# Order of the stick-breaking heads and the square root in a two-layer hybrid block: values placed behind the next block's first scores

## The chip, the cores and the metric

One Trainium2 chip, one core. The metric is the device time of one execution, in microseconds (us); lower is better. The engines are PE (TensorE; its weight loads are PEld), DVE (VectorE), ACT (ScalarE), POOL (GpSimd) and SP (SyncE, which here only issues transfers).

## The reference, cut to what matters

A two-layer model on 528 tokens (16 of them "meta" tokens) of width 1024. Layer 0 mixes with a state-space group and retention, layer 1 with stick-breaking attention and a gated linear recurrence; a convolutional feed-forward part follows each. The change is in the mixer of layer 1:

```python
def stick_breaking_attention(q, k, v):            # 16 heads of 64
    ...
        z = jnp.einsum('bqhd,bkhd->bhqk', q, k) * scale
        strict = jnp.arange(s1)[None, :] < jnp.arange(s0, s1)[:, None]
        log_1m = jnp.where(strict, jax.nn.log_sigmoid(-z), 0.0)
        after = lax.cumsum(log_1m, axis=3, reverse=True) - log_1m
        w = jnp.where(strict, jnp.exp(jax.nn.log_sigmoid(z) + after), 0.0)
        outs.append(jnp.einsum('bhqk,bkhd->bqhd', w, v))

def rg_lru(x, w_a, b_a, w_x, b_x, lam):           # 8 blocks of 128 channels
    r = sigmoid(x @ w_a + b_a); i = sigmoid(x @ w_x + b_x)
    log_a = -LRU_C * r * softplus(-lam)
    a = exp(log_a)
    b = jnp.sqrt(jnp.maximum(-jnp.expm1(2.0 * log_a), 0.0)) * (i * x)
    # h_t = a_t * h_(t-1) + b_t over the tokens

u = h @ w_in;  q, k, v, gate, xr = split_cols(u, ...)
y = concat([attention, rg_lru(conv(xr)) * gelu(gate)]) @ w_out
```

## The kernel before

Activations are kept transposed, channels on partitions and the 528 tokens along the free dimension. Every dense product is done in three passes, high part times high part, high times low and low times high. A **unit** is one 128-column block of a weight: SP brings it to `raw`, ACT writes its rounded part to `whi` (L661), DVE the rest to `wlo` (L1059), and PE multiplies it in `gemm` (L359) in eight **portions** of six matmuls (the index k). There are two buffers of each of these, so the ACT copy for unit u waits (in `split_hi`) until PE has finished unit u-2, and signals it only with the last matmul of that unit.

Layer 1's mixer runs in eight **blocks** n = 0 to 7. A block has two attention heads (e = 0, 1) and one 128-channel block of the recurrence. While PE multiplies the five units of the next block's projection (the five tiles q, k, v, gate, xr), the function `l1_small(i, b, unit, k)` puts the small products of this block behind given portions; (3, 1) means behind portion 1 of unit 3. PE executes all this in one fixed order. Before the change it is:

- (0, 2): `suffix(n-1, 1)`, the triangular sums of the second head of the block before (L549 to L561). They need the high and low parts that ACT and DVE make one after the other (`soft` on both engines).
- (0, 5): `values(n-1)`: the weights of both heads times the values (L571 for the 16 meta tokens, L576 for the rest), into bank 3 and a corner of bank 1 of the shared PSUM tile `small` (`sp_`).
- (0, 7): `gates(n)` (L586, L588), the two gate products of the recurrence.
- (1, 3): `v_out(n)` (L595, L597), transposing the values; then `scores(n, 0)` (L403, and the mask products of L537), the scores of the first head, into banks 0 to 2.
- (3, 1): `suffix(n, 0)`. (3, 4): `scores(n, 1)`.

ACT's order in a block, written out in `l1_block`: weight copy 1 (`split(1)`), `weigh(n-1, 1)` (L948, the exponential of the second head before), `l1_heads_out(n-1)` (L980, L981, results of `values` to `yT`), `lru_root(n-1)` (a table load and a square root at L995, and `load_exp` at L942, another table load with a one-column exponential), `l1_gates(n)` (L956 to L964), weight copy 2, `l1_v(n)` (L969, transposed values to `sv_tok`), then `soft(n, 0)`. In `soft` the absolute value and the exponential of the scores come first (L920 to L925), then what is called `between` (for the first head `l1_v_last` at L973 and weight copy 3, for the second weight copy 5), then a table load and the logarithms (L927, L929), then the high parts (L934 to L938). `load_exp`, `weigh(n, 0)`, weight copy 4, `soft(n, 1)` and `load_exp` end the block.

DVE's order: tile 4, the four-tap convolution for the recurrence (`lru_in`, L1096 and L1098), the low part of weight 1, `lru_out(n-1)` (L1577 to L1579, needs the square root), `gelu_in` (L1556 to L1558), the low part of weight 2, tile 0, weight 3, tile 1, `soft(n, 0)` (L1502 to L1529), `lru_var` (L1563 to L1567), and so on. `l1_gates(n)` waits for `lru_out(n-1)`, because they share buffers, and `v_out(n)` waits for the first part of `l1_gates(n)`.

In block 7 (`early=True`) the units beside it are those of the output projection; their right-hand side is made by `y_part` (ACT L835, DVE L1381) in the buffers `hn_hi` and `hn_lo`, with `weigh(6, 1)` inside it, and PE waits for it portion by portion. `suffix(7, 1)` and `values(7)` stand in the sixth unit of that projection.

Of the kernel before, what the change touches and what calls it, by code (L numbers as in the profile page):

```python
# [21 lines left out]
P = 128  # L22
# [14 lines left out]
NT = 5  # L37
# [10 lines left out]


V_LAST = ((1, 416), (2, 432))  # L50

# [68 lines left out]
def build(nc, x_h, vec_h, cst_h, dec_h, w_dt, w_ssd, w_ret, w_out0, w_fi0, w_fo0, w_l1, w_out1, w_fi1, w_fo1,  # L122
# [4 lines left out]
    with ctx:  # L127
# [3 lines left out]
        def sem(name):  # L131
            return ctx.enter_context(nc.semaphore(name))
# [24 lines left out]
        with scope() as mix:  # L157
# [38 lines left out]
            with scope() as s3:  # L196
                qs = [sb(f"qs{s}", [P, T], f32, s3) for s in range(2)]
                ks = [sb(f"ks{s}", [P, T], f32, s3) for s in range(2)]
                vs, gt, xc, tr = vr[:, 0, :], vr[:, 1, :], gr[:, 0, :], gr[:, 1, :]
                ubx = ub[:, 0, :]  # L200
                gw = [sb(f"gw{s}", [P, 2 * P], f32, s3) for s in range(2)]
                sv_tok = sb("sv_tok", [P, NT, P], f32, s3)
                lbuf = sb("lbuf", [P, CAUSAL], f32, s3)
                spb = sb("spb", [P, CAUSAL], f32, s3)
                sp_hi = sb("sp_hi", [P, CAUSAL], f32r, s3)
                sp_lo = sb("sp_lo", [P, CAUSAL], f32r, s3)
                later = sb("later", [P, LATER], f32, s3)


                spare = slice(KD * P, KH * P)  # L210
                later_hi = (whi[0][:, spare], sb("later_hi", [P, 416], f32r, s3)[:], whi[1][:, spare])
                later_lo = (wlo[0][:, spare], sb("later_lo", [P, 416], f32r, s3)[:], wlo[1][:, spare])
                wts = [sb(f"wts{s}", [P, CAUSAL], f32, s3) for s in range(2)]
                lt, lb = (sb(n, [P, T], f32, s3) for n in ("lt", "lb"))
                ge, ti, la = ub[:, 1, 3:3 + T], sq[:, 0, :], sq[:, 1, :]
                hb = sb("hb", [P, 2, 8], f32, s3)
                nsp = sb("nsp", [P, 8], f32, s3)
                nspt = sb("nspt", [P, 8], f32, s3)
# [20 lines left out]
        def pcol(name, c=0, n=1, rows=P):  # L239
# [36 lines left out]
            sem(n) for n in ("xc_done", "gates_done", "tri_done", "la_done", "lb_done", "root1_done"))  # L276
        z_done, l_done, spf_done, suf_done, w_done, pv_done = (
            sem(n) for n in ("z_done", "l_done", "spf_done", "suf_done", "w_done", "pv_done"))
        tvs_done, svtok_done, ysb_done, gu_done, gth_done, ylru_done = (
            sem(n) for n in ("tvs_done", "svtok_done", "ysb_done", "gu_done", "gth_done", "ylru_done"))  # L280
        sum_done, sphi_done, later_done, lathi_done, latlo_done = (
            sem(n) for n in ("sum_done", "sphi_done", "later_done", "lathi_done", "latlo_done"))
        prep_done, spl_done, spl_ln = sem("prep_done"), sem("spl_done"), sem("spl_ln")
# [63 lines left out]
        def _(pe):  # L347
# [181 lines left out]
            project(W_FO0, T_FO0, hid_hi, hid_lo, KH, (hlo_done, 0))  # L529


            def scores(n, b, e):

                rows = slice(HEAD * e, HEAD * (e + 1))
                causal([ks[b][rows, :]], [qs[b][rows, :]], None, once=True)
                for j, _, _, bk, c0, _ in (PIECES[0], *PIECES[2:]):
                    ins = pe.matmul(sp_[0:SZ[j], bk, c0:c0 + SZ[j]], ident_b[0:SZ[j], 0:SZ[j]],  # L537
                                    never[0:SZ[j], 0:SZ[j]], start=False, stop=True, skip_group_check=True)
                ins.then_inc(z_done, 1)
# [22 lines left out]
                                    stop=True, skip_group_check=True)  # L562
                ins.then_inc(suf_done, 1)

            def values(n):


                pe.wait_ge(w_done, 2 * n + 2)
                for e in range(2):
                    c = slice(HEAD * e, HEAD * (e + 1))  # L570
                    pe.matmul(sp_[c, 1, 32:32 + N_META], sv_tok[:, 0, c], wts[e][:, 0:N_META], start=True, stop=True)  # L571
                for j in range(NT):
                    q0 = max(N_META, P * j)
                    for e in range(2):
                        c = slice(HEAD * e, HEAD * (e + 1))
                        ins = pe.matmul(sp_[c, 3, q0 - N_META:512], sv_tok[0:SZ[j], j, c],  # L576
                                        wts[e][0:SZ[j], OFF[j] + q0 - P * j:OFF[j] + WJ[j]], start=j == 0,
                                        stop=j == NT - 1, skip_group_check=True)
                ins.then_inc(pv_done, 1)

            def gates(n, b, half_n):
                wait_count(pe, ysb_done, n)
                pe.wait_ge(xc_done, n + 1)
                pe.wait_ge(gw_in[b], 16 * (half_n + 1))
                for gate, (b0, b1, c1) in enumerate(((0, 1, 0), (2, 1, 16))):
                    pe.matmul(sp_[:, b0, 0:512], gw[b][:, gate * P:(gate + 1) * P], xc[:, 0:512],  # L586
                              start=True, stop=True)
                    ins = pe.matmul(sp_[:, b1, c1:c1 + 16], gw[b][:, gate * P:(gate + 1) * P], xc[:, 512:T],  # L588
                                    start=True, stop=True)
                ins.then_inc(gates_done, 1)  # L590

            def v_out(n):

                for i in range(4):
                    pe.transpose(sp_[:, 3, P * i:P * (i + 1)], vs[:, P * i:P * (i + 1)], ident)  # L595
                for e, (bk, c0) in enumerate(V_LAST):
                    ins = pe.matmul(sp_[0:SZ[4], bk, c0:c0 + HEAD], vs[:, 512:T], ident[:, HEAD * e:HEAD * (e + 1)],  # L597
                                    start=True, stop=True)
                ins.then_inc(tvs_done, 1)

            def l1_small(i, b, unit, k):

                n = 2 * i + b
                before = not (isinstance(n, int) and n == 0)
                if (unit, k) == (0, 2) and before:
                    suffix(n - 1, 1)
                if (unit, k) == (0, 5) and before:
                    values(n - 1)
                if (unit, k) == (0, 7):
                    gates(n, b, i)  # L610
                if (unit, k) == (1, 3):
                    pe.wait_ge(tri_done, n + 1)
                    v_out(n)
                    scores(n, b, 0)
                if (unit, k) == (3, 1):
                    suffix(n, 0)
                if (unit, k) == (3, 4):
                    pe.wait_ge(w_done, 2 * n + 1)
                    scores(n, b, 1)

# [19 lines left out]
            for c in range(5, 8):  # L640
                def after(k):
                    if c == 5 and k == 2:
                        suffix(7, 1)
                    if c == 5 and k == 5:
                        values(7)
                hgemm(At(0, 0, W_OUT1 + c), At(0, 0, T_OUT1 + c), after=after)

            project(W_OUT1 + KD, T_OUT1 + KD, y_hi, y_lo, KD, (ylo_done, 3 * KD), per=1)
# [6 lines left out]
        def _(act):  # L655
# [257 lines left out]
            act.activation(nspt[:], nspt[:], ACT.Ln, bias=1.0).then_inc(spl_ln, 1)  # L913
            act.wait_ge(spl_done, 2)

            def soft(n, e, between):


                act.wait_ge(z_done, 2 * n + e + 1)
# [7 lines left out]
                act.activation(lbuf[0:SZ[4], FULL:CAUSAL], lbuf[0:SZ[4], FULL:CAUSAL], ACT.Ln, bias=1.0)  # L927
                for b, w, at in reversed(BANKS):
                    act.activation(lbuf[:, at:at + w], lbuf[:, at:at + w], ACT.Ln, bias=1.0).then_inc(l_done, 1)  # L929

                for k, (b, w, at) in enumerate(reversed(BANKS)):
                    act.wait_ge(sum_done, 3 * (2 * n + e) + k + 1)
# [30 lines left out]
                act.wait_ge(gu_done, n + 1)  # L963
                act.activation(ge, ge, ACT.Tanh, scale=GELU_C).then_inc(gth_done, 1)  # L964

            def l1_v(n):
                act.wait_ge(tvs_done, n + 1)
                wait_count(act, pv_done, n)
                act.activation(sv_tok[:, 0:4, :], sp_[:, 3, :].rearrange("p (i c) -> p i c", c=P), ACT.Copy)  # L969

            def l1_v_last(n):
                for e, (bk, c0) in enumerate(V_LAST):
                    ins = act.activation(sv_tok[0:SZ[4], 4, HEAD * e:HEAD * (e + 1)], sp_[0:SZ[4], bk, c0:c0 + HEAD],  # L973
                                         ACT.Copy)
                ins.then_inc(svtok_done, 1)

            def l1_heads_out(n):

                act.wait_ge(pv_done, n + 1)
                act.activation(yT[:, n, 0:N_META], sp_[:, 1, 32:32 + N_META], ACT.Copy)  # L980
                act.activation(yT[:, n, N_META:T], sp_[:, 3, :], ACT.Copy).then_inc(ysb_done, 1)  # L981

            def hb_col(gate, n):
# [14 lines left out]
            def l1_block(i, b, early=False):  # L998
# [7 lines left out]
                if early:  # L1006
                    act.wait_ge(unit_done, W_OUT1)
                    y_part(hn_hi, EARLY[1], W_OUT1, lambda: weigh(n - 1, 1))
                else:
                    split(1)  # L1010
                    if before:
                        weigh(n - 1, 1)
                if before:
                    l1_heads_out(n - 1)
                    lru_root(n - 1)
                l1_gates(n)
                split(2)
                l1_v(n)
                soft(n, 0, lambda: (l1_v_last(n), split(3)))
                load_exp()  # L1020
                weigh(n, 0)
                split(4)
                soft(n, 1, lambda: split(5))
                load_exp()

            for b in range(2):
                l1_block(0, b)
# [6 lines left out]
            l1_block(3, 1, early=True)  # L1034
            split_hi(At(0, 0, W_OUT1 + 6))
            weigh(7, 1)
            l1_heads_out(7)
            lru_root(7)
            split_hi(At(0, 0, W_OUT1 + 7))
            split_hi(At(0, 0, W_OUT1 + 8))  # L1040
            act.wait_ge(ysb_done, 8)
# [740 lines left out]
```

## Time and profile before

| | us |
|---|---|
| three runs, median (lowest, highest) | 1885.35 (1885.19, 1885.55) |
| the profiled execution | 1886.69 |
| its span | 1884.7 |
| PE busy | 1825.9 (97%) |
| DVE busy | 1221.8 (65%) |
| ACT busy | 755.5 (40%) |

The blocks of layer 1's mixer run from 1020 to 1430 us of the span. A timeline row gives the start, the time busy, the engine, the line, the operation with its output and inputs, the count of instructions merged in it, and in brackets how long the engine was idle before it and what it is taken to have waited for. A matmul's end is modelled and overlaps the next, so lengths on PE are best read from start to start.

### The profile page before, as it was taken

How to read it: one execution, taken by the hardware profiler on the slowest of the kernel's cores; microseconds unless marked ns; L12 is line 12 of the kernel's file. 1: busy time of each engine (PE TensorE's matmuls, PEld its weight loads, DVE VectorE, ACT ScalarE, POOL GpSimd, SP SyncE). 2: the span in 40 equal slices, each digit the busy share in tenths (PEclk: the TensorE clock that was granted, in tenths of full speed). 3: DMA queues.
4: the chain of work that ended last, by engine and by line, in shares of the span. 5: the costliest groups of instructions: out<-in, count | busy, mean ns of one | idle time of the engine just before them, and what ended most of it. 6: DMA issues, size and time to landing. Idle time of an engine off the chain costs nothing.

```text
span 1884.7 us, 36044 instructions
## 1 busy us (share of the span) xinstructions
PE 1825.9 (97%) x14286; PEld 1737.0 (92%) x14286; DVE 1221.8 (65%) x1740; ACT 755.5 (40%) x1135; POOL 68.5 (4%) x140
## 2 busy tenths in 40 slices
PE   7999999999999999999999999999899999999996
PEld 7999998999899999999998888888789999999996
DVE  7787756455456777774334777777775688878323
ACT  5444432121234222222224777777774422223221
POOL 0122220000000000000000000000000000000000
PEclk9999999999999999999999999999999999999998
DMA  4222213222222222232222111111112222223221
GB/s 150 91 80 79 90 49 111 68 68 67 68 71 86 89 89 89 89 97 95 90 78 72 58 59 49 59 58 59 57 45 79 89 89 89 89 89 102 93 92 60
DMA packets 39938, 149.92 MB, mean 80 GB/s; under 512 B 4384, under 2 KB 5408, under 8 KB 39216
## 3 DMA queue, kind: packets, MB, share of 16 engines
q1 hardware_dynamic: 38672, 142.16, 24.1%
q10 hardware_dynamic: 1184, 6.60, 1.0%
q8 instruction: 59, 0.97, 0.2%
q14 instruction: 23, 0.19, 0.0%
HBM read 146.62 MB, written 2.13 MB: 79 GB/s over the span
## 4 chain that ended last, share of the span: by engine, by line
PE 71%; issue 12%; DVE 9%; ACT 6%; POOL 2%; DMA 0%; DVEq 0%; ACTq 0%; POOLq 0%
PE gp L359 60%; PE small L403 3%; PE small L414 3%; DVE spb L1502 1%; DVE sp_lo L1524 1%; ACT lbuf L922 1%; DVE wlo L1059 1%; ACT lbuf L925 1%; PE small L576 1%; POOL dec L1664 1%; PE small L553 1%; ACT whi L661 1%; PE small L561 1%; ACT L927 1%; ACT L995 0%
## 5 line engine op out<-in xcount | busy, mean ns | idle before, releaser
L359 PE MATMUL gp<-hn_hi,whi 128*128 128x264 f32 x3216 | 664.6, 288 | 23.0 <-DVE wlo L1059 12.2
L359 PE MATMUL gp<-hn_hi,wlo 128*128 128x264 f32 x3216 | 657.4, 286 | 0.0
L359 PE MATMUL gp<-hn_lo,whi 128*128 128x264 f32 x3216 | 656.7, 286 | 0.0
L661 ACT ACTIVATE whi<-raw 128x1024 fp32r<-128x1024 f32 (+1 forms) x249 | 273.6, 1099 | 775.5 <-PE gp L359 774.5
L1059 DVE TENSOR_TENSOR wlo<-raw,whi 128x1024 fp32r<-128x1024 f32 (+1 forms) x249 | 317.5, 1275 | 390.1 <-ACT whi L661 389.6
L359 PEld LDWEIGHTS gp<-hn_hi,whi 128*128 128x128 f32 x3216 | 503.0, 189 | 29.2 <-DVE wlo L1059 14.2
L359 PEld LDWEIGHTS gp<-hn_hi,wlo 128*128 128x128 f32 x3216 | 500.7, 189 | 0.0
L359 PEld LDWEIGHTS gp<-hn_lo,whi 128*128 128x128 f32 x3216 | 500.3, 189 | 0.0
L359 PE MATMUL gp<-hid_hi,whi 128*128 128x264 f32 x704 | 142.6, 284 | 0.0
L359 PE MATMUL gp<-hid_lo,whi 128*128 128x264 f32 x704 | 142.5, 284 | 0.0
L359 PE MATMUL gp<-hid_hi,wlo 128*128 128x264 f32 x704 | 142.5, 283 | 0.0
L359 PEld LDWEIGHTS gp<-hid_lo,whi 128*128 128x128 f32 x704 | 109.1, 188 | 0.0
L359 PEld LDWEIGHTS gp<-hid_hi,whi 128*128 128x128 f32 x704 | 109.0, 188 | 0.0
L359 PEld LDWEIGHTS gp<-hid_hi,wlo 128*128 128x128 f32 x704 | 108.7, 188 | 0.0
L1098 DVE SCALAR_TENSOR_TENSOR cu<-ubf,vec,cu 128x528 f32<-128x528 f32 x88 | 67.6, 769 | 11.6 <-DVE cu L1096 3.1
L1098 DVE SCALAR_TENSOR_TENSOR cg<-ubf,vec,cg 128x528 f32<-128x528 f32 x88 | 67.7, 769 | 11.4
L1089 DVE TENSOR_TENSOR ubf<-gp,rstd 128x528 f32<-128x528 f32 x88 | 62.3, 708 | 13.7 <-DVE wlo L1059 8.7
L671 ACT ACTIVATE sq<-hT 128x528 f32<-128x528 f32 (+1 forms) x40 | 25.7, 643 | 93.6 <-DVE hT L1389 93.5
L359 PE MATMUL gp<-y_hi,whi 128*128 128x264 f32 x256 | 52.6, 286 | 4.1 <-DVE y_lo L1381 4.1
L414 PE MATMUL small<-x_dt,dec 128*128 128x64 f32 (+2 forms) x480 | 50.3, 257 | 2.5 <-DVE dec L1176 2.5
L1389 DVE TENSOR_TENSOR hT<-gp,hT 128x528 f32<-128x528 f32 (+1 forms) x48 | 33.9, 707 | 28.9 <-PE gp L359 24.1
L414 PEld LDWEIGHTS small<-x_dt,dec 128*128 128x128 f32 (+2 forms) x480 | 45.8, 159 | 6.9 <-DVE dec L1176 3.3
(241 smaller groups left out, 1907.1 us busy)
## 6 DMA issues: line engine op xcount, KB each, us to landing
raw<-in SPq DMA_DIRECT2D x217, 512.0 KB, 3.6
raw<-in SPq DMA_DIRECT2D x32, 704.0 KB, 4.1
cs_bc<-cs_scratch ACTq DMA_DIRECT2D x4, 1056.0 KB, 6.2
hT<-in SPq DMA_DIRECT2D x4, 528.0 KB, 7.4
out<-yT SPq DMA_DIRECT2D x4, 512.0 KB, 2.8
rdec<-in ACTq DMA_DIRECT2D x1, 1056.0 KB, 8.9
gw<-in SPq DMA_DIRECT2D x8, 128.0 KB, 3.4
rope<-in ACTq DMA_DIRECT2D x1, 528.0 KB, 5.8
```

The lines of the kernel that those rows point to most:

```text
L359: ins = pe.matmul(gp[t.par][:, h, 0:H2], wp[w.par][:, cols], rp[:, k0 + k, h * H2:(h + 1) * H2], start=first and k == 0 and n == 0, stop=l ...
L403: ins = pe.matmul(sp_[0:SZ[j], b, c0:c0 + n], kk[:, P * j:P * j + SZ[j]], qq[:, q0:q0 + n], start=(d == 0) if not once else c0 == 0, stop= ...
L414: ins = pe.matmul(dst(i), wt[0:SZ[j], at:at + SZ[i]], val(j), start=j == 0, stop=j == i)
L553: pe.matmul(sp_[:, bk, c0:c0 + w], neg_r[:, 0, :], sp_lo[:, at:at + w], start=False, stop=True, skip_group_check=True)
L561: ins = pe.matmul(sp_[:, bk, c0:c0 + w], neg_r[:, 1, :], later_lo[part][:, 0:w], start=False, stop=True, skip_group_check=True)
L576: ins = pe.matmul(sp_[c, 3, q0 - N_META:512], sv_tok[0:SZ[j], j, c], wts[e][0:SZ[j], OFF[j] + q0 - P * j:OFF[j] + WJ[j]], start=j == 0, st ...
L661: act.activation(whi[w.par][:, 0:kt * P], raw[w.par][:, 0:kt * P], ACT.Copy).then_inc(hi_done, 1)
L671: act.activation(sq[:, s, :], hT[:, m, :], ACT.Square).then_inc(sq_done, 1)
L1059: ve.tensor_tensor(wlo[w.par][:, n], raw[w.par][:, n], whi[w.par][:, n].bitcast(f32), ALU.subtract).then_inc(lo_done, 1)
L1089: ins = ve.tensor_tensor(dst, gout(t.par), halves(rstd[:]), ALU.mult)
L1098: ins = ve.scalar_tensor_tensor(dst, src[:, k:k + T], w0(k), dst, ALU.mult, ALU.add)
L1389: ve.tensor_tensor(halves(hT[:, m, :]), gout(t.par), halves(hT[:, m, :]), ALU.add)\
```

## The change

The values of block n-1 move from (0, 5) of block n to (1, 3), behind `scores(n, 0)`; their part for the meta tokens (`values_first`) goes inside `scores`, ahead of the mask products, to other columns of bank 1. The rest waits for a new semaphore, `svmain_done`, that ACT raises in `l1_v(n)`. `sv_tok` is doubled. `gates(n)` waits for `weigh(n-1, 1)` and no longer for the copying out of the values. `suffix(n, 0)` goes from (3, 1) to (3, 0) and `scores(n, 1)` from (3, 4) to (3, 3). On ACT, `weigh(n-1, 1)` comes ahead of weight copy 1, `l1_heads_out(n-1)` goes behind the logarithms of `soft(n, 0)`, its small part into `between`, and `lru_root(n)` takes the place of the last `load_exp` of block n.

```diff
-                sv_tok = sb("sv_tok", [P, NT, P], f32, s3)
+                sv_tok = [sb(f"sv_tok{s}", [P, NT, P], f32, s3) for s in range(2)]
...
-            def scores(n, b, e):
+            def scores(n, b, e, behind=None):
                 rows = slice(HEAD * e, HEAD * (e + 1))
                 causal([ks[b][rows, :]], [qs[b][rows, :]], None, once=True)
+                if behind is not None:
+                    behind()
...
-            def values(n):
+            def values_first(n, b):
                 pe.wait_ge(w_done, 2 * n + 2)
                 for e in range(2):
-                    c = slice(HEAD * e, HEAD * (e + 1))
-                    pe.matmul(sp_[c, 1, 32:32 + N_META], sv_tok[:, 0, c], wts[e][:, 0:N_META], start=True, stop=True)
+                    c = head_rows(e)
+                    pe.matmul(sp_[c, 1, FIRST], sv_tok[b][:, 0, c], wts[e][:, 0:N_META], start=False, stop=True,
+                              skip_group_check=True)
...
             def gates(n, b, half_n):
-                wait_count(pe, ysb_done, n)
+                wait_count(pe, w_done, 2 * n)
...
             def v_out(n):
+                wait_count(pe, ysb_done, n - 1)
...
                 if (unit, k) == (0, 2) and before:
                     suffix(n - 1, 1)
-                if (unit, k) == (0, 5) and before:
-                    values(n - 1)
                 if (unit, k) == (0, 7):
                     gates(n, b, i)
                 if (unit, k) == (1, 3):
                     pe.wait_ge(tri_done, n + 1)
                     v_out(n)
-                    scores(n, b, 0)
-                if (unit, k) == (3, 1):
+                    scores(n, b, 0, (lambda: values_first(n - 1, 1 - b)) if before else None)
+                    if before:
+                        pe.wait_ge(svmain_done, n + 1)
+                        values(n - 1, 1 - b)
+                if (unit, k) == (3, 0):
                     suffix(n, 0)
-                if (unit, k) == (3, 4):
+                if (unit, k) == (3, 3):
                     pe.wait_ge(w_done, 2 * n + 1)
                     scores(n, b, 1)
...
             def soft(n, e, between, behind=None):
...
                 for b, w, at in reversed(BANKS):
                     act.activation(lbuf[:, at:at + w], lbuf[:, at:at + w], ACT.Ln, bias=1.0).then_inc(l_done, 1)
+                if behind is not None:
+                    behind()
...
-                    split(1)
                     if before:
                         weigh(n - 1, 1)
-                if before:
-                    l1_heads_out(n - 1)
-                    lru_root(n - 1)
+                    split(1)
                 l1_gates(n)
                 split(2)
-                l1_v(n)
-                soft(n, 0, lambda: (l1_v_last(n), split(3)))
+                l1_v(n, b)
+
+                def between():
+                    l1_v_last(n, b)
+                    if before:
+                        l1_first_out(n - 1)
+                    split(3)
+
+                soft(n, 0, between, (lambda: l1_heads_out(n - 1)) if before else None)
                 load_exp()
                 weigh(n, 0)
                 split(4)
                 soft(n, 1, lambda: split(5))
-                load_exp()
+                lru_root(n)
...
             weigh(7, 1)
+            act.wait_ge(pv_done, 8)
+            l1_first_out(7)
             l1_heads_out(7)
-            lru_root(7)
```

## Rows read from the trace of the kernel before

**Rows 1.** Waits of PE over the span: us in total, times, longest.
```profile
PE small L553 <- DVE sp_lo L1524: 5.4, 15, 0.5
PE small L595 <- ACT sq L957: 5.0, 7, 0.9
```

**Rows 2.** Timeline of PE, from the second scores of block 2 to block 3.
```profile
1146.26 0.51 PE L359 MATMUL gp<-hn_hi,whi 128*128 128x264 f32 x2
...
1159.61 0.40 PE L359 MATMUL gp<-hn_hi,whi 128*128 128x264 f32 x2
...
1162.03 2.65 PE L576 MATMUL small<-wts,sv_tok 128*64 128x512 f32 x20
1164.62 0.51 PE L359 MATMUL gp<-hn_hi,whi 128*128 128x264 f32 x2
...
1166.18 1.02 PE L586 MATMUL small<-gr,gw 128*128 128x512 f32 x2
...
1168.26 0.49 PE L359 MATMUL gp<-hn_hi,whi 128*128 128x264 f32 x2
...
1172.32 0.66 PE L595 MATMUL small<-cst,vr 128*128 128x128 f32 x4 [0.89 <-ACT sq L957]
...
1176.45 0.52 PE L359 MATMUL gp<-hn_hi,whi 128*128 128x264 f32 x2
...
1186.81 0.82 PE L549 MATMUL small<-sp_hi,neg_r 128*128 128x432 f32 x3
...
1190.03 0.41 PE L359 MATMUL gp<-hn_hi,whi 128*128 128x264 f32 x2
```

**Rows 3.** Timeline of ACT, same stretch.
```profile
1157.86 1.28 ACT L942 ACT_TABLE_LOAD   x1
...
1165.56 1.28 ACT L995 ACT_TABLE_LOAD   x1
...
1168.81 0.20 ACT L942 ACTIVATE idle_a<-eps_col 128x1 f32<-128x1 f32 x1
1170.66 0.69 ACT L956 ACTIVATE gr<-small,hb 128x512 f32<-128x512 f32 x1 [1.65 <-DVE yT L1579]
...
1175.45 0.60 ACT L969 ACTIVATE sv_tok<-small 128x512 f32<-128x512 f32 x1
...
1179.74 1.06 ACT L661 ACTIVATE whi<-raw 128x1024 fp32r<-128x1024 f32 x1
...
1190.23 1.42 ACT L948 ACTIVATE wts<-small 128x512 f32<-128x512 f32 x3 [0.45 <-PE small L561]
```

**Rows 4.** Timeline of DVE, same stretch.
```profile
1161.48 1.68 DVE L1098 SCALAR_TENSOR_TENSOR gr<-ub,vec,gr 128x528 f32<-128x528 f32 x2 [0.15 <-DVE gr L1098]
1163.07 1.22 DVE L1059 TENSOR_TENSOR wlo<-raw,whi 128x1024 fp32r<-128x1024 f32 x1
1167.60 0.71 DVE L1577 TENSOR_TENSOR lb<-lb,sq 128x528 f32<-128x528 f32 x1 [3.30 <-ACT lb L995]
...
1188.82 0.55 DVE L1529 TENSOR_TENSOR wlo<-later,whi 128x384 fp32r<-128x384 f32 x1
```

**Rows 5.** Timeline of block 7, PE and DVE.
```profile
1357.73 0.78 PE L359 MATMUL gp<-hn_hi,whi 128*128 128x264 f32 x2 [6.14 <-DVE hn_lo L1381]
...
1364.88 0.41 PE L359 MATMUL gp<-hn_hi,whi 128*128 128x264 f32 x2
...
1369.72 1.57 DVE L1098 SCALAR_TENSOR_TENSOR gr<-ub,vec,gr 128x528 f32<-128x528 f32 x2
...
1377.13 0.66 PE L595 MATMUL small<-cst,vr 128*128 128x128 f32 x4 [0.42 <-ACT sq L957]
```

**Rows 6.** Timeline behind block 7, ACT and PE.
```profile
1415.60 0.15 ACT L949 ACTIVATE wts<-small 16x16 f32<-16x16 f32 x1
1415.84 0.29 PE L571 MATMUL small<-wts,sv_tok 128*64 128x16 f32 x4
```

**Rows 7.** Busy time, granted clock, DMA share in one window.
```profile
1358.00:1362.00 4.00, 4.00 (x19) 4.00 (x19) 3.97 (x6) 2.57 (x4) 0.00 (x0) 0.50 0.09 14
```

More of the change, by code:

```diff
@@ L50 @@
 V_LAST = ((1, 416), (2, 432))
+FIRST = slice(480, 480 + 16)
 LATER1, LATER2, LATER3, LATER = 528, 928, 1200, 1216
@@ L278, in build @@
             sem(n) for n in ("z_done", "l_done", "spf_done", "suf_done", "w_done", "pv_done"))
-        tvs_done, svtok_done, ysb_done, gu_done, gth_done, ylru_done = (
-            sem(n) for n in ("tvs_done", "svtok_done", "ysb_done", "gu_done", "gth_done", "ylru_done"))
+        tvs_done, svmain_done, svtok_done, ysb_done, gu_done, gth_done, ylru_done = (
+            sem(n) for n in ("tvs_done", "svmain_done", "svtok_done", "ysb_done", "gu_done", "gth_done", "ylru_done"))
         sum_done, sphi_done, later_done, lathi_done, latlo_done = (
@@ L563, in suffix, with head_rows, values @@
                 ins.then_inc(suf_done, 1)
-            def values(n):
+            def head_rows(e):
+                return slice(HEAD * e, HEAD * (e + 1))
+            def values_first(n, b):
                 pe.wait_ge(w_done, 2 * n + 2)
                 for e in range(2):
-                    c = slice(HEAD * e, HEAD * (e + 1))
-                    pe.matmul(sp_[c, 1, 32:32 + N_META], sv_tok[:, 0, c], wts[e][:, 0:N_META], start=True, stop=True)
+                    c = head_rows(e)
+                    pe.matmul(sp_[c, 1, FIRST], sv_tok[b][:, 0, c], wts[e][:, 0:N_META], start=False, stop=True,
+                              skip_group_check=True)
+            def values(n, b):
                 for j in range(NT):
@@ L574, in values @@
                     for e in range(2):
-                        c = slice(HEAD * e, HEAD * (e + 1))
-                        ins = pe.matmul(sp_[c, 3, q0 - N_META:512], sv_tok[0:SZ[j], j, c],
+                        c = head_rows(e)
+                        ins = pe.matmul(sp_[c, 3, q0 - N_META:512], sv_tok[b][0:SZ[j], j, c],
                                         wts[e][0:SZ[j], OFF[j] + q0 - P * j:OFF[j] + WJ[j]], start=j == 0,
@@ L644, in after @@
                     if c == 5 and k == 5:
-                        values(7)
+                        values_first(7, 1)
+                        values(7, 1)
                 hgemm(At(0, 0, W_OUT1 + c), At(0, 0, T_OUT1 + c), after=after)
@@ L914, in _, with soft @@
             act.wait_ge(spl_done, 2)
-            def soft(n, e, between):
+            def soft(n, e, between, behind=None):
                 act.wait_ge(z_done, 2 * n + e + 1)
@@ L964, in l1_gates, with l1_v, l1_v_last, l1_first_out @@
                 act.activation(ge, ge, ACT.Tanh, scale=GELU_C).then_inc(gth_done, 1)
-            def l1_v(n):
+            def l1_v(n, b):
                 act.wait_ge(tvs_done, n + 1)
-                wait_count(act, pv_done, n)
-                act.activation(sv_tok[:, 0:4, :], sp_[:, 3, :].rearrange("p (i c) -> p i c", c=P), ACT.Copy)
-            def l1_v_last(n):
+                wait_count(act, pv_done, n - 1)
+                act.activation(sv_tok[b][:, 0:4, :], sp_[:, 3, :].rearrange("p (i c) -> p i c", c=P),
+                               ACT.Copy).then_inc(svmain_done, 1)
+            def l1_v_last(n, b):
                 for e, (bk, c0) in enumerate(V_LAST):
-                    ins = act.activation(sv_tok[0:SZ[4], 4, HEAD * e:HEAD * (e + 1)], sp_[0:SZ[4], bk, c0:c0 + HEAD],
+                    ins = act.activation(sv_tok[b][0:SZ[4], 4, HEAD * e:HEAD * (e + 1)], sp_[0:SZ[4], bk, c0:c0 + HEAD],
                                          ACT.Copy)
                 ins.then_inc(svtok_done, 1)
+            def l1_first_out(n):
+                act.activation(yT[:, n, 0:N_META], sp_[:, 1, FIRST], ACT.Copy)
             def l1_heads_out(n):
                 act.wait_ge(pv_done, n + 1)
-                act.activation(yT[:, n, 0:N_META], sp_[:, 1, 32:32 + N_META], ACT.Copy)
                 act.activation(yT[:, n, N_META:T], sp_[:, 3, :], ACT.Copy).then_inc(ysb_done, 1)
```

## Prediction

> **What bounds the kernel now.** I read the page first: PE is busy 97% of the span, so an edit pays only where it removes a wait of PE, or a matmul. This one removes no matmul. Next the list of PE's waits, in which layer 1's mixer has two: at the transposed values and inside the triangular sums [rows 1]. Then I followed one block on PE's timeline, from the resumption behind one second-head score to the next event of each kind, and beside it ACT and DVE [rows 2 to 4]. I count from two origins. Origin A is 1146.26, where PE resumes portions behind `scores(n-1, 1)`; origin B is 1176.45, behind `scores(n, 0)`.
>
> Measures from these rows. 14 portions lie between 1176.45 and 1186.81, 0.74 us each. The main part of `values` takes 1164.62 - 1162.03 = 2.59, the gates 1168.26 - 1166.18 = 2.08, `v_out` with the first scores 1176.45 - 1172.32 = 4.13. `suffix` takes 1190.03 - 1186.81 = 3.22. Its last three matmuls can only start when DVE's last low part is there, at 1188.82 + 0.55 = 1189.37, and PE goes on 0.66 later. Its columns, 4896, at the pace of a portion (1584 columns in 0.74) are 2.3 us, so about 0.9 of each suffix is waiting for the chain from scores over ACT and DVE [rows 2, 4]. What the list shows as waits is only part of it.
>
> **From origin A (block n's gates and transposed values), before.** The suffix ends at +13.35 (1159.61), the transposed values start at +26.06 (1172.32), and B lies at +30.19 [rows 2].
>
> After the change, step by step. `scores(n, 1)` comes one portion earlier, so 15 portions lie ahead of `suffix(n, 1)`: PE is there at 11.10, needs 2.3, and DVE's chain still allows the end at +13.35 only: the extra portion lies in what was waiting. Five portions, with no `values` among them: gates due at 17.05. They need two things. The weights: ACT finishes its high parts at 1157.86 (+11.60), and then comes `lru_root`. That sequence took 1165.56 to 1169.01, 3.45 [rows 3], where `load_exp` alone took 1.28 + 0.20, so ACT is free at +15.05 and the exponential of 1.42 and its small piece end near +16.5. And the convolution, which ends at 1161.48 + 1.68 (+16.90) [rows 4]. Both are just in time. The gates end at +19.13 and four portions of unit 1 bring PE to the transposed values at +22.09.
>
> They wait for the gates' tanh, that waits for `lru_out`, and this one now stands behind another thing than the square root: weight 1. ACT copies it after the exponential, 1.06, until +17.5; DVE makes its low part, 1.22 [rows 4], until +18.75 (unit 1 needs it at +19.13: hidden, with 0.4 to spare). From the start of `lru_out` to ACT's tanh it is 1170.66 - 1167.60 = 3.06, from there to PE 1172.32 - 1170.66 = 1.66 [rows 2 to 4], so PE starts at +23.47. The wait that the change aims at stays, 1.4 long. The 4.13 and 0.14 for the two small meta products put B at +27.74. Against 30.19 that is **-2.45**, in which 2.59 us of `values` have left this stretch.
>
> **From origin B (first head), after.** `values` is now the first thing. It waits for ACT's copy of the values, which ended 1175.45 + 0.60 - 1172.32 = 3.73 behind the start of `v_out` [rows 2, 3]; B is at 4.27, so no stall. But `values` stands in unit 1, ahead of its last four portions, and ACT's weight copy 3, inside `soft(n, 0)`, waits until unit 1 is done. It started at 1179.74 (B+3.29) [rows 3]. Now unit 1 ends at 2.59 + 4 x 0.74 = 5.55, and ACT sees it 0.20 later (that was the lag between PE's end of the suffix at 1190.03 and the exponential at 1190.23 [rows 2, 3]): B+5.75, **2.46 later**. Table load, logarithms, DVE's sums and low parts, all follow that copy one behind the other, so DVE's last low part, and with it the end of the suffix, moves by the same 2.46, from +13.58 to +16.04. PE reaches the suffix at 2.59 + 13 x 0.74 = 12.21 and could end it at 14.5; it waits the rest. `l1_first_out` and the copying out of the heads (0.8 us on ACT) stand where ACT waits anyway, for unit 1 and for DVE. Three portions and the second scores follow as before: **+2.46**.
>
> So a regular block is even: the values leave one stretch and return in the other, the root's wait shrinks by nothing, and the cover that the values should give the first head's chain is eaten by the weight copy behind them.
>
> **Block 7 and behind it.** The new `lru_root(6)` stands ahead of `y_part`, for which PE has stood idle 6.14 [rows 5]; it adds 3.45 - 1.49 = 1.96 to that. From the suffix's end, 1364.88 + 1.96, five portions reach the gates at 1370.5, but the convolution, behind DVE's part of `y_part`, ends at 1369.72 + 1.57 + 1.96 = 1373.25 [rows 5]. Before, the values filled that hole; now PE waits 2.8 there. Gates from 1373.3, 2.08, four portions: transposed values at 1378.35, where the tanh (1373.3 + 3.06 + 1.66 = 1378.0) doesn't hold them. Against 1377.13 that is +1.22, with the 0.14 **+1.36** at B, and then the +2.46 of this block. Behind it, `weigh(7, 1)` ended at 1415.75, `values(7)` began at 1415.84 [rows 6]: no slack, and `lru_root(7)` now stands ahead of that exponential: **+1.96**. What it used to cost behind the values was hidden: at that place PE had units 6 and 7 to do.
>
> **Sum.** Six stretches from A at -2.45 = -14.7; seven from B (blocks 1 to 7; block 0 has no values to place and stays as it is) at +2.46 = +17.2; +1.36 and +1.96. Together **+5.8**. On the profiled execution, 1886.69, that is 1892.5; on the median of the three runs, 1885.35, it is **1891.2**.
>
> Unknowns. The small meta products inside `scores` are in no row at that place: between 0 and 0.29 a block, I take 0.14. Gates that miss their two inputs by a little: from 0 to 0.5 a block, +3 in all; I take 0. A tanh that comes earlier because `lru_out` doesn't wait for weight 1's low part to the end: down to -1.4 a block, -8 in all, the whole wait; I take 0, as DVE's order fixes it.
>
> **A rule against the rows.** The root's move puts a table switch ahead of the second head's weights in every block. In this trace the whole sequence of two loads, square root and small exponential is 3.45 [rows 3]. The Trainium skill, ScalarE: Activation LUTs, section "What ACT_TABLE_LOAD costs", gives about 2.66 us for each switch, a load of 1283 ns and a drain. By it the one extra switch would cost 1.4 more wherever ACT has no slack, as an estimate 8 x 1.4 = 11 us more, near 1902. The trace's load agrees and the drain isn't there: two switches by the page alone exceed the 3.45 measured.
>
> **Rivals.**
> 1. *The first head's chain is covered after all*: the values hide it and weight copy 3 isn't held back. The suffix would end at B+14.5 in place of 16.0, 1.6 x 7 = 11 less: 5.8 - 11 gives -5, **1880**, faster. It decides by whether ACT's copy starts before B+4.2. For it speaks only that this wait (3.29) looks short now; against it, that the copy's signal comes from the last matmul of unit 1. Chance 0.13.
> 2. *Even*: regular blocks as computed or 0.3 better each (-2), and the two end terms are half given back, since the next stage starts on other work. About **1887**, between -3.7 and +3.7. Chance 0.27. Against it: PE is without slack in both places.
> 3. *The clock falls*. Behind the 6.14 idle the granted clock was 0.50 [rows 7], the lower level (1.2 of 2.4 GHz), and three portions and a suffix took 1364.88 - 1357.73 = 7.15 where 3 x 0.74 + 3.22 = 5.44 is the rule: 1.7 a fall. The new 2.8 before block 7's gates could do it once (1893), the waits of 1.4 and 1.5 in each block seven times more (1905). Waits of 0.9 before didn't. Chance 0.10, nearly all for the single one.
> 4. My forecast, 0.50.
>
> The measurement tells 0.2% (3.8 us) from no change: faster, below 1881.6, 0.13; within, 0.27; slower, above 1889.1, 0.60. The range runs from 1882 to 1897, leaving out rival 1 and repeated clock falls.
>
> **What would show it.** Right: ACT's weight copy 3 idle before it, waiting for PE, some 2 us in seven blocks; PE's wait inside the first head's suffix grows to over 1 us; the wait at the transposed values is about 1.4, and DVE's `lru_out` follows weight 1's low part without a gap and with no wait for the root; 7 to 8 us idle before block 7, near 3 before its gates, 2 before `values(7)`. Wrong: a copy 3 that starts at B+3.3, a first suffix that ends near B+14, or stalls before the gates in every block.

## The result, and the profile after

The changed kernel is slower. Four runs gave 1896.70 us in the median (1892.85 to 1900.57) against 1885.27 (1884.42 to 1885.55): ratio 1.0056, 95% interval 1.0037 to 1.0075. A second set later gave 1895.46 against 1885.92, ratio 1.0054 (1.0036 to 1.0072). The profiled execution took 1892.85, its span is 1890.8, 6.1 above the span before.

The stretch that the change touches, from block 0's gates to the end of `values(7)`, went from 398.78 (1019.78 to 1418.56) to 408.66 (1016.12 to 1424.78): +9.9. The span shows only 6.1 of it, because this execution had reached the stretch 3.7 earlier, in code that is the same in both. That is chance and not the change: over the ten profiles of this document the stretch starts anywhere from 1015.4 to 1022.0. Of the 3.7, 2.2 were there by 993; where they come from wasn't traced. The other 1.5 came with TensorE's clock. Before, it was at its lower level (1.2 of 2.4 GHz) for part of the start of layer 1, in the changed kernel not. Windows of the kernel before, then after (columns as in rows 7):

```profile
994.00:1000.00 6.00, 5.31 (x31) 5.32 (x32) 2.47 (x3) 0.46 (x1) 0.00 (x0) 0.72 0.61 159
```
```profile
994.00:1000.00 6.00, 6.00 (x52) 6.00 (x51) 1.19 (x3) 1.07 (x1) 0.00 (x0) 1.00 0.46 163
```

PE's waits after. The wait at the transposed values is longer (5.8, before 5.0 [rows 1]), the one before block 7 too (7.6 at the longest, before 6.14 [rows 5]), and the wait for ACT's weights at `values(7)` is new:

```profile
PE gp L360 <- DVE hn_lo L1402: 10.3, 4, 7.6
PE small L605 <- ACT sq L971: 5.8, 6, 1.0
...
PE small L552 <- ACT sp_hi L949: 3.7, 8, 0.5
PE small L556 <- DVE sp_lo L1545: 3.7, 8, 0.5
...
PE small L576 <- ACT wts L963: 1.8, 1, 1.8
PE small L595 <- issue: 1.8, 1, 1.8
```

The block of rows 2 on PE's timeline. L595 are the gates here, L605 the transposed values, L576 the meta part of the values, L585 the rest, L552 the first triangular sums:

```profile
1143.42 0.51 PE L360 MATMUL gp<-hn_hi,whi 128*128 128x264 f32 x2
...
1157.03 0.41 PE L360 MATMUL gp<-hn_hi,whi 128*128 128x264 f32 x2
...
1160.69 1.08 PE L595 MATMUL small<-gr,gw 128*128 128x512 f32 x2
...
1162.83 0.49 PE L360 MATMUL gp<-hn_hi,whi 128*128 128x264 f32 x2
...
1167.04 0.66 PE L605 MATMUL small<-cst,vr 128*128 128x128 f32 x4 [1.02 <-ACT sq L971]
...
1171.40 2.67 PE L585 MATMUL small<-wts,sv_tok 128*64 128x512 f32 x20
1174.00 0.51 PE L360 MATMUL gp<-hn_hi,whi 128*128 128x264 f32 x2
...
1184.69 0.50 PE L552 MATMUL small<-sp_hi,neg_r 128*128 128x512 f32 x1 [0.50 <-ACT sp_hi L949]
...
1187.59 0.40 PE L360 MATMUL gp<-hn_hi,whi 128*128 128x264 f32 x2
```

ACT beside it. The square root stands ahead of the weights (L962), and ahead of weight copy 3 (L673 at 1177.30) ACT is idle 2.47, waiting for PE (2.45 to 2.49 in all seven blocks):

```profile
1155.29 1.28 ACT L1011 ACT_TABLE_LOAD   x1
1156.59 0.65 ACT L1011 ACTIVATE lb<-lb 128x528 f32<-128x528 f32 x1
1157.25 1.28 ACT L956 ACT_TABLE_LOAD   x1
1158.55 0.20 ACT L956 ACTIVATE idle_a<-eps_col 128x1 f32<-128x1 f32 x1
1158.66 1.40 ACT L962 ACTIVATE wts<-small 128x512 f32<-128x512 f32 x3
...
1165.39 0.69 ACT L970 ACTIVATE gr<-small,hb 128x512 f32<-128x512 f32 x1 [4.35 <-DVE yT L1600]
...
1177.30 1.06 ACT L673 ACTIVATE whi<-raw 128x1024 fp32r<-128x1024 f32 x1 [2.47 <-PE gp L360]
```

DVE: `lru_out` (L1598) follows weight 1's low part at once and waits for no root (before 3.30 [rows 4]):

```profile
1161.07 1.23 DVE L1080 TENSOR_TENSOR wlo<-raw,whi 128x1024 fp32r<-128x1024 f32 x1 [0.48 <-ACT whi L673]
1162.33 0.71 DVE L1598 TENSOR_TENSOR lb<-lb,sq 128x528 f32<-128x528 f32 x1
...
1186.38 0.55 DVE L1550 TENSOR_TENSOR wlo<-later,whi 128x384 fp32r<-128x384 f32 x1
```

Behind block 7 PE waits 1.85 for the weights, and the values then take 4.3 in place of 2.65, the granted clock having fallen. Timeline and windows of the changed kernel:

```profile
1420.43 0.29 PE L576 MATMUL small<-wts,sv_tok 128*64 128x16 f32 x4 [1.85 <-ACT wts L963]
1420.57 4.29 PE L585 MATMUL small<-wts,sv_tok 128*64 128x512 f32 x20
```
```profile
1418.00:1422.00 4.00, 2.15 (x15) 1.06 (x16) 3.00 (x3) 2.34 (x5) 0.00 (x0) 0.91 0.18 29
1422.00:1426.00 4.00, 4.00 (x26) 2.44 (x23) 0.89 (x2) 0.68 (x2) 0.00 (x0) 0.66 0.28 107
```

### The profile page after: what moved, and what is told of

Read it like the earlier page. It is cut to its first block, busy times and chain, and to the rows that moved or that the text cites. A ratio compares the mean times of both kernels' runs of the same rounds, so it can differ in the third digit from the quotient of the medians.

```text
span 1890.8 us, 36037 instructions
## 1 busy us (share of the span) xinstructions
PE 1823.8 (96%) x14286; PEld 1734.7 (92%) x14286; DVE 1221.8 (65%) x1740; ACT 743.6 (39%) x1119; POOL 67.8 (4%) x140
## 4 chain that ended last, share of the span: by engine, by line
PE 74%; issue 10%; DVE 8%; ACT 6%; POOL 1%; DMA 0%; ACTq 0%; DVEq 0%; POOLq 0%
PE gp L360 63%; PE small L404 4%; PE small L415 3%; DVE spb L1523 1%; DVE wlo L1080 1%; PE small L585 1%; ACT whi L673 1%; POOL dec L1685 1%; DVE sp_lo L1545 1%; ACT L956 1%; ACT L1011 1%; ACT L939 1%; ACT wts L962 1%; DMA rdec<-in 0%; PE small L556 0%
## 5 line engine op out<-in xcount | busy, mean ns | idle before, releaser
L673 ACT ACTIVATE whi<-raw 128x1024 fp32r<-128x1024 f32 (+1 forms) x249 | 273.9, 1100 | 794.0 <-PE gp L360 793.6
L360 PE MATMUL gp<-y_lo,whi 128*128 128x264 f32 x256 | 52.1, 285 | 0.0
```

Of the source, the lines that this page charges most:

```text
L360: ins = pe.matmul(gp[t.par][:, h, 0:H2], wp[w.par][:, cols], rp[:, k0 + k, h * H2:(h + 1) * H2], start=first and k == 0 and n == 0, stop=l ...
L673: act.activation(whi[w.par][:, 0:kt * P], raw[w.par][:, 0:kt * P], ACT.Copy).then_inc(hi_done, 1)
```

## The experiments

Each was run beside the kernel before, and is an edit to the changed kernel unless it says otherwise. "Stretch" is block 0's gates to the end of `values(7)` in the profiled execution (before 398.8); "falls" counts the blocks among 1 to 6 in it where TensorE's clock fell to its lower level while the small matmuls ran. R is the ratio of the times to the kernel before, with its interval.

| kernel | median (range), runs | kernel before | R | stretch | falls |
|---|---|---|---|---|---|
| changed | 1896.7 (1892.9-1900.6), 4 | 1885.3 | 1.0056 (1.0037-1.0075) | 408.7 | 0 |
| e7, the same again | 1895.5 (1892.0-1900.6), 6 | 1885.9 | 1.0054 (1.0036-1.0072) | 408.5 | 0 |
| e1, values in unit 2 | 1888.2 (1883.6-1898.7), 12 | 1887.5 | 1.0007 (0.9991-1.0023) | 408.8 | 4 |
| e2, root behind copy 1 | 1888.6 (1884.0-1890.0), 10 | 1887.5 | 1.0005 (0.9996-1.0014) | 401.0 | 0 |
| e3, both | 1876.0 (1873.2-1879.6), 5 | 1887.5 | 0.9939 (0.9926-0.9953) | 389.4 | 0 |
| e4, root alone on before | 1903.9 (1900.6-1905.8), 4 | 1887.5 | 1.0081 (1.0067-1.0096) | 415.6 | 4 |
| e5, e3 and one portion later | 1874.4 (1873.0-1876.5), 6 | 1885.9 | 0.9937 (0.9921-0.9952) | 386.6 | 0 |
| e6, e1 and two portions later | 1882.0 (1881.1-1885.2), 12 | 1885.9 | 0.9980 (0.9970-0.9990) | 394.9 | 0 |
| e8, root late at the ends | 1892.0 (1888.7-1902.5), 12 | 1888.0 | 1.0022 (1.0012-1.0031) | 412.4 | 3 |

**Values out of unit 1 (e1).** The edit to the changed kernel:

```diff
                     scores(n, b, 0, (lambda: values_first(n - 1, 1 - b)) if before else None)
-                    if before:
-                        pe.wait_ge(svmain_done, n + 1)
-                        values(n - 1, 1 - b)
+                if (unit, k) == (2, 0) and before:
+                    pe.wait_ge(svmain_done, n + 1)
+                    values(n - 1, 1 - b)
```

> The changed kernel with one edit: the values of the block before stand behind portion 0 of unit 2 in place of portion 3 of unit 1, so unit 1 ends, and weight copy 3 can start, without waiting for them. Theory A (the copy behind unit 1 holds the first head's chain): ACT's copy 3 starts 3.3 to 3.5 us behind the first scores in place of 5.8, the first head's suffix ends near 14.5 us behind them in place of 16.2, about 1.7 less in each of seven blocks, 12 less than the changed kernel: 1884 to 1886. Theory B (the suffix is late because two heads' copying out and the extra portion moved out of this stretch delay it): the suffix still ends at 16 and the time stays near 1896.

Timelines of PE and ACT in a block without a fall, from the resumption behind the first scores to the end of the suffix:

```profile
1326.57 0.51 PE L360 MATMUL gp<-hn_hi,whi 128*128 128x264 f32 x2
...
1329.90 1.04 ACT L673 ACTIVATE whi<-raw 128x1024 fp32r<-128x1024 f32 x1
...
1339.00 0.78 PE L552 MATMUL small<-sp_hi,neg_r 128*128 128x432 f32 x3
...
1341.22 0.41 PE L360 MATMUL gp<-hn_hi,whi 128*128 128x264 f32 x2
```

Copy 3 starts 3.33 behind the scores and the suffix ends at 14.65, where the changed kernel has 5.90 and 16.19 (1171.40 to 1177.30 and 1187.59). Theory A holds. The five lowest runs, 1883.6 to 1885.6, are the expected time, with a mean granted clock of 0.993 to 0.994. The median lies above it, and the four highest, 1893.9 to 1898.7, have 0.986 to 0.987: there the clock falls. The profile is one of these four. A block of this kernel with a fall, on PE and in windows:

```profile
1169.21 0.66 PE L605 MATMUL small<-cst,vr 128*128 128x128 f32 x4 [1.03 <-ACT sq L971]
...
1170.12 4.12 PE L404 MATMUL small<-qs,ks 64*128 64x512 f32 x12
```
```profile
1168.00:1174.00 6.00, 4.96 (x20) 2.87 (x18) 2.71 (x5) 4.78 (x9) 0.00 (x0) 0.79 0.02 9
1174.00:1178.00 4.00, 4.00 (x25) 3.70 (x25) 0.49 (x1) 2.71 (x6) 0.00 (x0) 0.50 0.43 131
```

The scores took 4.12, elsewhere 2.86. One fall costs 5.8 - 4.36 = 1.4 from the start of the transposed values to the resumption behind the scores (without a fall 27.89 - 23.53 = 4.36), and 21.7 - 20.16 = 1.5 from there to the resumption behind the second scores, 3 in all.

**The root behind weight copy 1 (e2), and both edits (e3).** The edit of e2 to the changed kernel (the last root stands behind the copying out of block 7's heads):

```diff
                     split(1)
+                if before:
+                    lru_root(n - 1)
                 l1_gates(n)
...
                 soft(n, 1, lambda: split(5))
-                lru_root(n)
+                load_exp()
```

> The changed kernel with the square root (and its two table loads) taken from the end of the block to behind weight copy 1 of the next one; behind block 7's values for the last. Theory A (the root ahead of the second head's weights costs at the ends): idle time before block 7 falls from 7.6 to 5.6, the wait before values(7) of 1.9 goes, and with it the low clock that followed; the wait at the transposed values falls from 1.4 to about 0.8 in six blocks. Together 3.6 + 2 + 3.5, about 9 less than the changed kernel: 1886 to 1888. Theory B (the root's place is neutral, as the waits at the transposed values come from the order on DVE alone): under 3 less.

PE's wait at the transposed values in the same block is 0.47, `values(7)` starts without one, and the values behind it take 2.65:

```profile
1166.50 0.66 PE L605 MATMUL small<-cst,vr 128*128 128x128 f32 x4 [0.47 <-ACT sq L971]
...
1415.53 2.65 PE L585 MATMUL small<-wts,sv_tok 128*64 128x512 f32 x20
```

From the ratios it is 9.6 less than the changed kernel (0.0051 of 1887.5), theory A. Its profiled stretch is only 7.7 less. There the clock fell at block 7's gates, behind the wait of 1.8 (granted 0.78 from 1366 to 1370), and gates and the four portions behind them took 6.77 in place of 5.16: 1.6, without which it would be 9.3.

> Both edits: values behind portion 0 of unit 2, square root behind weight copy 1. If the two losses are independent they add: 12 + 9 less than the changed kernel, 1874 to 1877, faster than the kernel before by 0.5%. If the ACT engine becomes the limit, less than the larger of the two.

With 1876.0 it is 0.6% faster than the kernel before. The stretch falls by 19.3. Alone, e2 takes 9.3 from it, its fall at the gates left out, and e1 11.9 (408.7 - 408.8 + 4 falls of 3). Both hold the 1.6 that the changed kernel's slow `values(7)` cost, since the clock didn't fall there in either profile; counted once, they make 19.6. The two losses add up, and ACT isn't a new limit.

**The root alone, on the kernel before (e4).** The last `lru_root(7)` goes too.

```diff
                     l1_heads_out(n - 1)
-                    lru_root(n - 1)
...
                 soft(n, 1, lambda: split(5))
-                load_exp()
+                lru_root(n)
```

> The kernel before with one edit: the square root takes the place of the last load_exp of each block, the values stay in unit 0. Theory A (the root ahead of the second head's weights is late for whatever needs them): the wait of 0.9 at the transposed values goes, but PE waits 1 to 2 us for the weights ahead of values in six blocks, and 2 more before block 7 and before values(7): 8 to 11 more than before, 1893 to 1896. Theory B (what the edit aims at: only the wait at the transposed values matters): 5 less, 1880.

The wait at the transposed values is gone (in this kernel L595; it carries none), but PE waits for the second head's weights, and a fall follows:

```profile
1218.61 0.29 PE L571 MATMUL small<-wts,sv_tok 128*64 128x16 f32 x4 [2.01 <-ACT wts L949]
1218.75 4.32 PE L576 MATMUL small<-wts,sv_tok 128*64 128x512 f32 x20
...
1229.65 0.60 PE L595 MATMUL small<-cst,vr 128*128 128x128 f32 x4
```

Seven such waits make 13.2 us. The values took 4.2 to 4.3 in four of the blocks 1 to 6 and behind block 7, 2.6 elsewhere: 8.3 in all of the 16.9 by which the stretch grew. The rest is the 8 to 11 expected; the time, 15 above, wasn't, as the clock stood in neither theory.

**Filling the wait (e5, e6).** e5 is e3, and e6 is e1, with this line changed to (1, 4) and (1, 5):

```diff
-                if (unit, k) == (1, 3):
+                if (unit, k) == (1, 4):
```

> As both edits (values behind portion 0 of unit 2, root behind weight copy 1), and the transposed values with the first scores behind portion 4 of unit 1 in place of 3. Theory A (PE waits 0.8 there for a tanh whose time DVE fixes, and the first head's suffix has cover to spare): the portion fills the wait, 0.7 less in each of six to seven blocks and little back at the suffix, 4 to 5 less than with both edits alone: 1871 to 1873. Theory B (the portion is only missed at the suffix of the first head): no change, 1876.

The wait at the transposed values leaves the list. From the resumption behind the first scores to that behind the second it is now 19.43 (1168.32 to 1187.75), with e3 20.16. Over blocks 1 to 6 e5 is 3.5 shorter; blocks 0 and 7, with no such wait to fill, give 0.7 back, which leaves 2.8. The medians differ by 1.5, but they were taken beside different runs of the kernel before, and by the ratios only 0.4 is left (0.0002 of 1886). Both are less than expected, and the intervals overlap. The profile shows theory A's mechanism; the times decide for neither. It has the lowest median of all, but e3 and e5 can't be told apart.

> The first experiment's kernel (values in unit 2, root still at the block's end) with the transposed values and first scores behind portion 5 of unit 1: two portions fill the wait there. It tells the wait from the clock. Theory A (the single runs of 1894 to 1899 of the first experiment come from the clock falling to its lower level behind waits of 0.9): no wait, no fall in a regular block, all runs within 4 us of each other, near 1878 to 1882, the six waits' own 0.9 to 1.4 given partly back at the suffix. Theory B (the clock falls because the small matmuls of scores and values stand close together): falls stay, and so does a spread of 10 us.

The median, 1882.0, is at the upper end of what was expected, and the twelve runs lie within 4.1 us, e1's within 15. Theory A, but for one fall left in block 0 of the profiled execution, behind a longer wait in its suffix (2.07). Timeline and window of the block shown for e1: no wait, scores of 2.86, the clock at its upper level.

```profile
1167.22 0.60 PE L605 MATMUL small<-cst,vr 128*128 128x128 f32 x4
1168.08 2.86 PE L404 MATMUL small<-qs,ks 64*128 64x512 f32 x12
```
```profile
1167.00:1177.00 10.00, 10.00 (x75) 7.04 (x74) 3.10 (x4) 8.91 (x16) 0.00 (x0) 1.00 0.17 52
```

So the small matmuls by themselves don't bring the fall: scores and values stand closer together here than in e1. In none of the ten profiles did the clock fall in blocks 1 to 6 without a wait of 0.9 us or more just ahead; and behind such a wait it fell only sometimes. That the edit worked by the wait alone, and not by the new place of the matmuls, is the plain reading; no run separates the two. The Trainium skill, TensorE: Matmul & The Clock Gate, section "HAM oscillation — how this bites in real kernels", describes waits for transfers of some 3 to 5 us between bursts of matmuls, each of which brings the throttle back. This case agrees in kind and not in size: e1's falls came behind waits of 0.90 to 1.03 us, and in four of six blocks.

**The changed kernel again (e7), and its ends repaired (e8).**

> The changed kernel once more, for another profile and more times beside the kernel before on the same chip. Theory A (5.8 by its waits, the rest of the median by clock falls that not every execution has): the lowest runs lie 5 to 8 above the median of the kernel before, the highest 12 to 16 above, and the runs with a lower mean clock are the longer ones. Theory B (the whole difference is waits): every run 10 to 12 above.

The times are theory A's: runs from 6 to 15 above the median of the kernel before. Its other half isn't borne out: clock and time go together only loosely here (1891.95 at 0.993, 1900.6 at 0.991, and 1896.5 at 0.990). Both profiles of this kernel are of its shortest runs, so that there is none of a long one.

e8 calls `lru_root(6)` behind `y_part`, `lru_root(7)` behind `l1_heads_out(7)`, and leaves the rest as changed.

> The changed kernel, with the square root of the last two blocks alone put late: behind the right-hand side of the output projection for block 6, behind the copying out of the heads for block 7. Blocks 0 to 5 stay as changed. Theory A (the ends are a loss of their own): before block 7 PE idles 5.6 in place of 7.6, no wait before values(7), no low clock behind it: 1.2 to 2 and 3.7 less than the changed kernel, 5 in all, 1890 to 1892, and the rest of the loss, 4 to 5 over the kernel before, stays with the regular blocks. Theory B (the ends are absorbed by what follows them): under 1.5 less.

By the ratios it is 6 less than the changed kernel (0.0032 of 1888), theory A: the ends were over half of the loss by the ratios, and half of it in the profile (5.0 of 9.9). Its profiled execution is the longest of the twelve: three falls, at 3.0 each, 9 of the 13.6 by which its stretch exceeds the one before. What remains, 4.6, are the regular blocks.

## Why the prediction was right, and where its sizes were off

It said 1891.2 and slower; the median is 1896.7. The kernel is slower for the reasons given; the loss came out at 10 to 11 in place of 5.8. The range reached to 1897 and left repeated falls of the clock out, so that the median lies inside it by 0.3 us. The direction rests on mechanisms that the experiments show; that the number still fell inside was in part luck. The nearest thing to the forecast of 5.8, the 6.1 between the spans, is chance as well: it is the stretch's 9.9 less a start that was 3.7 early.

- **Origin A, predicted B at +27.74, -2.45 a block.** Measured 1171.40 - 1143.42 = 27.98 in the same block; over six blocks 167.3 against 180.8 before, -13.5 in place of -14.7. The transposed values start at +23.62 (predicted 23.47), behind the chain that the prediction named: weights, copy 1, its low part, `lru_out` without a wait, tanh. The meta products took 0.22, not 0.14. The wait there was 0.9 to 1.0 and not 1.4: the suffix took 2.5 and not 2.3 and ended at +13.61 (1157.03), and the gates started at +17.27, so PE came later to it. And the block shown was longer than the mean of the six before (30.19 to 30.13): a term multiplied from one row.
- **Origin B, predicted suffix end at +16.04, +2.46 a block.** Measured 16.19, from ACT's copy at +5.90 (5.75). The idle time that the profile shows in this suffix is 0.9 to 1.0 (before 0.4 to 0.5), where over 1 was expected. Over seven blocks +18.4 in place of +17.2. e1 shows it to be the copy's doing.
- **Block 7, +1.36.** Measured 1381.08 - 1341.82 = 39.26, before 38.02: +1.24. The wait before its unit 0 is 7.6 (the root added 1.4 and not 1.96), and before its gates there are 0.6 and 1.8 in place of 2.8 at once: the low parts of `y_part` come late too, and split it. The profile names no cause for the 1.8, but DVE's convolution ends at 1371.5 and the gates start at 1371.62.
- **`values(7)`, +1.96.** Here the term was too small: +3.8 from the last second scores on. The wait is 1.85, but the clock falls behind it and the values last 1.6 longer; the remaining 0.3 lies in the suffix and the portions. Rival 3 had priced one fall at 1.7, at block 7's gates, where none came in this kernel (in e2 one did, and cost 1.6); it came behind `values(7)`'s wait.
- **"So a regular block is even"**: the sum of both stretches is +4.9 over all blocks, and with the ends, 1.24 and 3.77, it makes the +9.9. Without the fall at `values(7)` 8.2 is left; predicted 5.8.
- **"Waits of 0.9 before didn't [let the clock fall]"** was the weak step. That came from one execution. Under the changed order the same wait, 0.9 to 1.05, let it fall in 0 of 6 blocks (two profiles), 3 of 6 (e8) and 4 of 6 (e1). Such falls are what spreads e1's runs. That they also make the changed kernel's median 4 us longer than its profiled run is argued from e1 and e8, and not shown: no long run of it was profiled, and the kernel before, whose waits at that place were 0.9 at most, spreads over 7 to 10 us too (1883.4 to 1890.8, 1882.1 to 1892.1).
- The rule of the Trainium skill on table switches (ScalarE: Activation LUTs, section "What ACT_TABLE_LOAD costs"), a drain behind each load: it takes 3.46 for two loads, root and exponential again (1155.29 to 1158.75), so the drain isn't there, and the 11 us more didn't come.

The rivals. The first (the chain is covered, 1880) is what e1 does once the copy is free. The second had the ends half given back; e8 gained 6 by mending them alone, more than the 3.3 predicted for them.

## What to carry to other kernels

Work put in as cover must not stand in front of something that feeds the chain it is to cover: here 2.6 us of matmuls ahead of a unit's last portions held back the buffer, by it a copy, and by it the whole chain; one unit further on the same matmuls gained 12 us (from e2 to e3). When a slow step is moved out of one queue position, look at what now stands behind it: the root left a wait of 0.9 and delayed weights that had next to no slack. And a wait of 1 us on TensorE cost 4 in this kernel wherever the clock fell behind it: its own 1, and 3 for the slower matmuls.

## Not expected of the hardware

The granted clock fell to its lower level behind waits of 0.9 to 1.05 us followed by transposes and scores (e1 in 4 of 6 blocks, e8 in 3 of 6), and behind waits of 1.9 on the average in five of seven (e4), not always in the same code. In the kernel before it fell at 994 us behind a wait of 2.5 us, in the changed kernel, behind the same wait in the same code, it didn't. Behind the wait of 1.84 before `values(7)` it fell in both profiles of the changed kernel and in e4, and not in e1 and e6. With the waits filled the runs came within 4.1 us (e6), without within 15 (e1).
